# Row-layout products of a fused two-block kernel: each product of 512 moving columns issued as two products of 256

## The reference

```
x = x + rms_norm(memory_attention(...) @ w_mo)          # "mo": 1024 x 1024
ffn = (gelu(gate) * val) @ w_down                        # "down": 2816 x 1024
o, z = u @ w_in[o columns], u @ w_in[z columns]          # "oz": 1024 x 4096
h = h + (h_heads * sigmoid(o) * silu(z)) @ w_out         # "lout": 2048 x 1024
```

## Time and profile before

| | before |
|---|---|
| median of 3 runs | 943.53 us |
| the profiled execution, its own time | 944.54 us |
| its span | 942.8 us |
| PE matmul busy | 930.5 us (99%), 7012 matmuls |
| weight loads busy | 865.8 us (92%) |
| VectorE busy | 656.5 us (70%) |
| ScalarE busy | 533.4 us (57%) |
| HBM traffic | 157.91 MB, mean 167 GB/s |

### The profile page before, as it was taken

The page is one execution under the profiler, slowest core; times in us unless marked ns, Lnnn a source line. Parts: engine busy times, 40 slices in busy tenths (PEclk is TensorE's granted clock), DMA queues, the critical chain, the costliest instruction groups (busy, mean ns, idle before and its releaser), DMA issues.

```text
span 942.8 us, 19167 instructions
## 1 busy us (share of the span) xinstructions
PE 930.5 (99%) x7012; PEld 865.8 (92%) x7012; DVE 656.5 (70%) x1115; ACT 533.4 (57%) x902; POOL 117.6 (12%) x111
## 2 busy tenths in 40 slices
PE   8999999999999999999999999999999999999997
PEld 7998899997999998879999999999999998888886
DVE  4888877555899887447877777765667475776643
ACT  6767676455766665445444444444563567666643
POOL 1200010000065453000111111111010000000000
PEclk9999999999999999999999999999999999999999
DMA  8843335435356556563555555555456354444561
GB/s 289 281 163 133 124 105 161 158 126 178 113 178 200 185 194 202 187 194 108 184 174 178 177 171 174 172 174 179 148 188 190 124 175 139 149 141 158 178 193 53
DMA packets 45075, 157.91 MB, mean 167 GB/s; under 512 B 6067, under 2 KB 7219, under 8 KB 44764
## 3 DMA queue, kind: packets, MB, share of 16 engines
q1 hardware_dynamic: 44524, 155.56, 50.4%
q0 software_dynamic: 496, 1.59, 0.6%
HBM read 156.06 MB, written 1.06 MB: 167 GB/s over the span
## 4 chain that ended last, share of the span: by engine, by line
PE 93%; DVE 3%; ACT 2%; issue 1%; DMA 1%; SPq 0%; DVEq 0%; ACTq 0%
PE acc L1238 13%; PE acc L1239 13%; PE acc L1240 13%; PE scores L1239 6%; PE scores L1238 6%; PE scores L1240 5%; PE acc L1193 4%; PE acc L1191 4%; PE acc L1192 4%; PE scores L1193 2%; PE scores L1191 2%; PE scores L1192 2%; PE outs L1193 2%; PE outs L1192 2%; PE outs L1191 2%; PE acc L1313 1%
## 5 line engine op out<-in xcount | busy, mean ns | idle before, releaser
L1792 DVE TENSOR_TENSOR w_lo<-raw,w_hi 128x1024 fp32r<-128x1024 f32 x288 | 353.8, 1234 | 102.0 <-ACT w_hi L602 101.3
L602 ACT ACTIVATE w_hi<-raw 128x1024 fp32r<-128x1024 f32 x288 | 302.3, 1056 | 160.5 <-PE acc L1240 69.4
L1238 PE MATMUL acc<-XH,w_hi 128*128 128x256 f32 (+1 forms) x624 | 179.0, 287 | 0.4 <-DVE XL L1898 0.4
L1239 PE MATMUL acc<-XL,w_hi 128*128 128x256 f32 (+1 forms) x624 | 177.6, 285 | 0.0
L1240 PE MATMUL acc<-XH,w_lo 128*128 128x256 f32 (+1 forms) x624 | 177.0, 284 | 0.0
L1239 PE MATMUL scores<-XL,w_hi 128*128 128x272 f32 (+1 forms) x424 | 120.9, 285 | 0.0
L1238 PE MATMUL scores<-XH,w_hi 128*128 128x272 f32 (+1 forms) x424 | 120.7, 285 | 0.0
L1240 PE MATMUL scores<-XH,w_lo 128*128 128x272 f32 (+1 forms) x424 | 120.4, 284 | 0.0
L1238 PEld LDWEIGHTS acc<-XH,w_hi 128*128 128x128 f32 x624 | 117.8, 189 | 2.8 <-issue 2.4
L1239 PEld LDWEIGHTS acc<-XL,w_hi 128*128 128x128 f32 x624 | 117.7, 189 | 0.1
L1240 PEld LDWEIGHTS acc<-XH,w_lo 128*128 128x128 f32 x624 | 117.4, 188 | 0.0
(11 more groups left out here) (524 smaller groups left out, 1775.7 us busy)
## 6 DMA issues: line engine op xcount, KB each, us to landing
raw<-weights SPq DMA_DIRECT2D x288, 512.0 KB, 3.5
cst<-params SPq DMA_DIRECT2D x1, 1080.5 KB, 10.7
XR<-x_t SPq DMA_DIRECT2D x2, 512.0 KB, 6.4
Y<-mem_t SPq DMA_DIRECT2D x1, 1024.0 KB, 9.4
AR<-bias_rows POOLq DMA_DIRECT2D x4, 256.0 KB, 6.3
out<-AR SPq DMA_DIRECT2D x2, 512.0 KB, 2.6
AR<-final_gain POOLq DMA_DIRECT2D x1, 512.0 KB, 7.3
cst<-params SPq DMA_DIRECT2D x1, 114.5 KB, 3.6
```

Source lines behind the costliest of these rows:

```text
L602: nc.scalar.activation(w_hi[:, n % SLOTS, :], raw[:, n % SLOTS, :], ACT.Copy).then_inc(hi_ready, 1)
L1238: nc.tensor.matmul(o, wh, h, start=start, stop=False)
L1239: nc.tensor.matmul(o, wh, l, start=False, stop=False)
L1792: V.tensor_tensor(w_lo[:, s, :], raw[:, s, :], w_hi[:, s, :].bitcast(F32), ALU.subtract).then_inc(lo_ready, 1)
```

## The change

Where `first` is given, the first of the three products stays whole. All others are issued as two: the first takes the 128-column blocks 0 and 2 of the 512 moving columns and writes blocks 0 and 2 of the bank, the second takes blocks 1 and 3. Both use the same stationary operand. The three kinds of product follow each other by a loop, with high by high first, then high by `w_lo`, then low by `w_hi`, as before. Nothing else is edited.

```
                 w = n % SLOTS
                 hi, lo = (p(j)[:, b * P:(b + 1) * P] for p in x)
+
+                def every_second(columns, q):
+
+                    return columns.rearrange("p (r q c) -> p q r c", r=2, q=2)[:, q]
+
                 c = slice((j % 2) * 512, (j % 2 + 1) * 512)
-                nc.tensor.matmul(o, hi, w_hi[:, w, c], start=first, stop=False)
-                nc.tensor.matmul(o, hi, w_lo[:, w, c], start=False, stop=False)
-                return nc.tensor.matmul(o, lo, w_hi[:, w, c], start=False, stop=last)
+                if first:
+                    nc.tensor.matmul(o, hi, w_hi[:, w, c], start=True, stop=False)
+                for part, x_part in ((w_hi, hi), (w_lo, hi), (w_hi, lo)):
+                    if first and part is w_hi and x_part is hi:
+                        continue
+                    for q in range(2):
+                        ins = nc.tensor.matmul(every_second(o, q), x_part, every_second(part[:, w, c], q), start=False,
+                                               stop=last and x_part is lo and q == 1)
+                return ins
```

## The result

The changed kernel takes 945.37 us (median of 22 runs, 944.93 to 946.35) against 943.65 us before (22 runs). The ratio is 1.0017, 95% interval 1.0011 to 1.0023: slower by 1.7 us, where I had forecast 4 us faster. The time lies inside my range; the direction is wrong.

The account below looks back on a forecast made before the run. PE's pace of starting products was taken as the only bound in the four stages; -4.6 us steady saving plus 0.6 us for beginnings gave -4.0, so 943.53 became 939.5 us, range 938.4 to 947.0.

Parts of the forecast that it names:

- What bounds the kernel: In the four stages mo, down, oz and lout, only how fast PE starts one product after another sets the time.
- The pace of what comes: Each split product in the four stages: two at 113.4 ns replace 231.8, saving 5.0 ns each, 4.6 us over 912.
- (a): `pair_tokens`: activations stationary, weights moving as two separate runs of 128; 113.4 ns a product, two 5.0 less than now.
- (d): `l_pv`: same stationary operand twice in a row, contiguous columns, alternating outputs; 120.9 ns a product, two 10.0 more than now.
- The comparison that was to decide, (a) against (b): Same column count and weight load, 3.4 ns apart; taken to show that runs of 128 leave less excess than contiguous columns.
- (b): The "up" stage: 256 contiguous moving columns; 116.8 ns a product, two 1.8 ns more than one whole product now.
- Rival 1: Fixed cost decides in the split stages; `pair_tokens` gains from its two slots, not its runs: 943.0 to 945.2 us, chance 0.30.
- (c): Compression stage: two runs of 128 past a stationary operand of 64 columns; 115.6 ns a product, two 0.6 less than now.
- The estimate from the Trainium skill's gap formula: Fixed gap of N/2.4 + 2.5 ns a product: 912 more products cost 2.3 us, nothing is gained, 945.8 us.
- Rival 2: In split products, the second on the same stationary operand is slower: up to 10.0 ns each, 9.1 us, 952.7; chance 0.20.
- Rival 3: A wait at each of 78 chunks costs 0.04 us, taking back 3.1 us: 942.0 us, within the forecast's range; no own chance.
- Beginnings: New starts of runs in mo, down, oz and lout, where something stands between: 15 x 0.04 = 0.6 us back.

Follow-up runs that it names:

- line 92 of the second kernel of products: Products alone, other engines idle: weights stationary, 256 columns moving from tiles 288 apart, beginning at 16; steady 116.7 ns a product.
- first kernel of products: Lines of 120 products alone, other engines idle, varying where the stationary operand begins and the form of columns and output; split form 114.1 ns at 16, 120.7 at 0.
- line 62: Products alone, other engines idle: split form, stationary at 16; the same code three times behind a small product took 114.2, 118.5 and 114.2 ns a product.

## Why the prediction was wrong

- *What bounds the kernel*: right. TensorE's pace alone sets the time of the four stages, in every run; nothing else became late, and neither the loads nor the conversions cost anything.
- *The count*: right, 912 more matmuls.
- *The pace of what comes*: this is the step that failed. I priced all 912 products by `pair_tokens` (a), since "the excess over one column per cycle goes mostly with the contiguous columns, and where the columns come as runs of 128 less of it is left". Contiguous halves go exactly as fast (945.37 us, all pieces to 0.02 us). What (a) had and "oz" and "lout" had not is a stationary operand that begins 16 columns past a multiple of 32 from the moving one. I compared rows (a) to (d) by shape and never by address, though the addresses stood in the code. Once the places are made equal, the forecast's -4.0 us comes out: the four stages take 4.0 us less and the kernel 0.9947 of the time before. That the number returns doesn't save its reason.
- *The comparison that was to decide, (a) against (b)*: its 3.4 ns are not the work of the runs, since contiguous columns reach 113.3 too. But they are not the distance modulo 32 either: (b) moves tiles at 16 + 288 k past weights at multiples of 128, a distance of 16 as in (a). The form of (b) alone has its 116.7 ns again (line 92 of the second kernel of products), and with tiles 256 apart 117.8 or 113.3. Why it does so stays open.
- *Rival 1* came nearest in time: 943.0 to 945.2. Its reason, the two slots, is wrong: the form of `pair_tokens` goes like the form in one slot at either distance. But its argument against me, that (c) has two runs and stays at 115.6, was a good one. Its stationary operands begin at multiples of 64, and I explained (c) away by its 64 columns. The place isn't all of it, since with 128 stationary columns this distance gave 120.0; no run had 64 of them, so (c) stays unexplained. The estimate from the Trainium skill's gap formula (TensorE: Matmul & The Clock Gate, section Back-to-back issue gap), 945.8, is near the measured 945.4, but not for its reason. That section calls the formula the gap of an isolated product, and for a stream of loads and products it gives some 131 ns at 512 columns; the lowest here is 226.7. In the runs, two split products at their right place go at 226.7 ns and a whole one at its own right place at 226.7 as well: no cost for each product is left.
- *Rival 2* (a second product on the same operand costs more): its price, up to 120.9 ns, is about what "oz" pays, its reason is not. A stationary operand of its own for each product changed nothing (114.2 at 16, 120.7 at 0, in the first kernel of products). Why (d) goes at 120.9 was not tested.
- *Rival 3* (a break at each chunk's wait): refuted. Chunks 9 and 10 of "down" each begin with a wait and go at a steady 226.7 ns for two split products, no gap at the 24th.
- *Beginnings*: I counted 0.04 us for each of 15. Steps of 117 to 124 ns do stand behind each beginning, and I missed one kind: each product kept whole because of `start=True` throws the stream out of its pace, so that the chunk with two of them in the second half of "down" goes at 231.2 instead of 226.7 ns. With the right places, four stages at a steady 226.7 would save 912 x 5.1 = 4.7 us, and 4.0 were measured: 0.7 for all beginnings, where I had 0.6.
- *The chances*: 0.50 for one row's pace was too much with three others beside it that disagreed and no known reason for the difference.

The Trainium skill (TensorE: Matmul & The Clock Gate, section Step-by-step: what each phase is for) says that the moving operand and the weight load have read ports of their own, so that loading the next weights takes nothing from the running matmul. No run here shows a port; but a pace that hangs on the distance of the two operands' addresses, 113.3 against 120.0 ns with all other engines idle, doesn't fit a load that takes nothing from the running product. What the two have in common, and why 16 columns (64 bytes) are the good distance for 256 columns and a multiple of 64 for 512, was not settled.

## What to carry to other kernels

Before a product's form is changed for the sake of its pace, look where its two operands begin in their partitions: here 16 fp32 columns of offset were worth 5% of the pace (120.0 against 113.3 ns), and the form nothing. The offset costs no work, but look at who else reads the moved tiles: `w_out` lost 0.3 us by it in two of the kernels. Price a new instruction by a row that equals it in address as well as in shape, and when two rows of one shape differ, don't choose one before the difference is explained. A function with several call sites is to be read site by site: the total of +1.7 us hid -1.6 and +3.5.

## What the runs showed of the hardware that I had not expected

Steady paces of fp32r products at the 2.4 GHz level, one core, other engines idle: 113.3 ns (sometimes 117.8) for 256 moving columns at distance 16, 120.0 at distance 0; 226.7 for 512 at a multiple of 64, 228.9 at 48, 232.4 at 32, 233.3 at 16.

Stages that no edit touches can differ in pace between two kernels. The stage that streams 272 columns is the same in both, and yet, before and after:

```profile
439.40 0.37 PE L1238 MATMUL scores<-XH,w_hi 128*128 128x272 f32 x1
...
672.99 0.29 PE L1240 MATMUL acc<-XH,w_lo 128*128 128x272 f32 x1
```

```profile
437.37 0.37 PE L1249 MATMUL scores<-XH,w_hi 128*128 128x272 f32 x1
...
670.53 0.29 PE L1251 MATMUL acc<-XH,w_lo 128*128 128x272 f32 x1
```

233.59 against 233.16 us. With the `lk` and `lq` stages behind it (122.3 against 121.3 ns a product over 347 steps) this makes 0.8 us, the main part of why the profiled spans differ by less than the medians. It isn't the change: the kernel with contiguous halves, identical to the changed one but for the columns, took 233.58 us for this stage, and the unsplit kernel with tiles at 0 took 233.16. Each kernel was profiled once, so it isn't shown whether this goes with the kernel or with the single execution. The two paces of line 62 above are the likely kind of cause; that they are the same thing was not shown.
